# First step of both MLPs' down product by seven half-size products, with another rotation of the weight slots

## The chip, the core and the metric

One NeuronCore of one Trainium2 chip runs the whole program. The time is device microseconds of one execution; lower is better. The engines are TensorE (PE in the profile; its weight loads are PEld), VectorE (DVE), ScalarE (ACT), GpSimd (POOL) and SyncE (SP), whose queue issues nearly all the DMAs.

## The reference, cut to what matters

A sequence of 512 tokens with 1024 features goes through two transformer layers (attention over selected keys, then gated linear attention), each with an MLP, and through a third layer with a gated MLP. All is float32. The change touches the two MLPs:

```python
def squared_relu_mlp(x, w_up, w_down):
    return jnp.square(jax.nn.relu(x @ w_up)) @ w_down      # w_up 1024 x 4096, w_down 4096 x 1024
...
        h = layer_norm(DN_ALPHA * h + squared_relu_mlp(h, mlp_w_up[i], mlp_w_down[i]), ln_mlp_g[i], ln_mlp_b[i])
```

A condition vector of the third layer, `silu(c) @ w_ada + b_ada` (1024 x 6144), doesn't depend on x. The kernel works it off piece by piece between other things.

## The kernel before, in words

**Precision.** Each float32 operand is split into a high part (a rounded copy, type float32r) and a low part (the rest). A product is three matmuls: high x high, low x high, high x low. ACT makes the high part, DVE the low part by a subtraction (`raw - high`). This holds for weights (`wh`, `wl`, 128x2048) and for the hidden activations (`uh`, `ul`).

**Weights.** All weights come in chunks of 1 MB, in the order of a list (`weight_plan`, L205). A chunk is fetched into one of three `raw` buffers in turn, and split into one of the weight slots 0 to 3 (`wh`/`wl` twice, `wh2`/`wl2`, `wh3`/`wl3`). Which slot is the plan's to say, by `slots(...)`. A condition chunk ("ada" in the code, `w_ada`) takes no slot: DVE multiplies it and adds it up into `acc` (L2235, L2238), and the table `ADA` says where in the list such chunks stand. Each engine walks the same list with a cursor. DVE's handles a pair (condition chunk, weight chunk) with the weights first.

**An MLP** has 8 steps n of 512 hidden columns. The up product of a step is two chunks (q = 0, 1) of 48 matmuls each, 128x512 (`gemm_T`, L765 to L767). ACT then applies relu and square to four tiles `rb` (128x512 f32, inside `A`). The down product of hidden step d runs on PE one step later, behind the up product of step d+1.

**The down product in seven products.** Steps d = 1 to 6 see their operands as 2 x 2 blocks and use seven products of half size, P1 to P7, instead of eight (`fold`, L935). PE takes them in the order P1, P2, P6, P5, P7, P4, P3, each with 12 matmuls (L960 to L962), so 84 in a step. The extra work is sums:
- of the hidden blocks, four in a row on POOL (`hidden_sums`, L3404; L3407, L3409, L3413, L3415), released by the low part of P1's operand. They overwrite `rb`, and ACT and DVE split their results for P6, P7, P5 and P3 (`high_of` L1619, `low_half_of` L2437);
- of the weight blocks, on DVE (`weight_sums`, `last_weight_sum`, L2451 to L2464). A step has four weight parts: X and Z are fetched, Y and W are the sums. P1 and P2 use X, P6 and P4 use Y, P5 uses W, P7 and P3 use Z;
- of the results: P1, P6 and P7 go into one chain of banks, and P6 may begin when DVE has added P1 to `h` (L2477), P7 when it has added P6. P4 and P5 keep their four banks from the first such step to the last.

**Step d = 0** was a plain product: `down_first` (L974 on PE, L2507 on DVE), 8 bank tiles of 12 matmuls, 96 in all (L986 to L988). DVE adds each tile to `ALPHA * h` (L2513) and prepares two rows of `h` for the steps to come (`corner`, L2504).

Before an MLP stands `cross`, which ends the product before and makes step n = 0 of the up product on the way. DVE also finishes the layer norm there: `affine` (L2353), eight operations on `h` and `gb`, 128x1024 f32, which the order written by hand spreads over DVE's work of the first two steps. POOL loads the next norm's gain and bias into `gb` once they are through (`load_two`, L3394).

The engines meet by semaphores only. Each engine's instructions run in the order in which its own program writes them.

Of the kernel before, what the change touches and what calls it, by code (L numbers as in the profile page):

```python
# [14 lines left out]
P = 128  # L15
T = 4
# [10 lines left out]
ADA = {0: [(0, 0, 0), (1, 0, 1), (1, 0, 1), (1, 0, 1), (1, 0, 1), (1, 0, 1), (1, 1, 1), (1, 1, 1)],  # L27
       1: [(0, 0, 0), (1, 1, 1), (0, 0, 1), (0, 0, 1), (0, 0, 1), (0, 0, 1), (0, 0, 1), (0, 0, 0)]}
# [176 lines left out]
def weight_plan(a_w_in, a_w_o, b_w_in, b_w_o, mlp_w_up, mlp_w_down, w_ada_2, w_in_2, w_out_2, w_gate_2, w_up_2, w_down_2):  # L205
# [5 lines left out]
    def slots(*numbers):  # L211
        turn[:] = numbers
# [58 lines left out]
    def plan_mlp(i):  # L271
        plan_up(i, 0)
        slots(2, 3, 0, 1)
        plan_up(i, 1)
        for c in range(2):
            plan(mlp_w_down[i], 0, 4, c * 512, 512)
            plan_adas((ADA[i][1][2] + 1 - c) // 2)
        for n in range(2, 8):
            own = 0 if n % 2 else 2
            slots(own, 3)  # L280
            plan_up(i, n)
            plan_fold("m%d" % (i + 1), n - 1, mlp_w_down[i], (n - 1) * 512, (2 - own, 1, own, 3), ADA[i][n][2])
        slots(2, 3)
        plan_down(i, 7)
# [58 lines left out]
def program(nc, x, positions, a_w_in, a_w_o, b_w_in, b_w_a2, b_b_a, b_g_norm, b_w_o, ln_mix_g, ln_mix_b,  # L343
# [4 lines left out]
    with ctx:  # L348
# [223 lines left out]
        STEPS = {"m1": (1, 6), "m2": (1, 6), "m3": (0, 3)}  # L572
# [16 lines left out]
        def freed(key, d, s):  # L589
# [3 lines left out]
            if key != "m3" and d == 1:  # L593
                return s_gemm.at((key, "u read", 0)) if s in FIRST else s_gemm.at(None)
# [98 lines left out]
        def tensor_program(pe):  # L693
# [280 lines left out]
            def down_first(key):  # L974
                for c in range(2):
                    i = cur.take(skip)
                    H, L, nk, ncol = parts(i)
                    w.wait_ge(*low_of(i))
                    w.wait_ge(*s_xlow.at((key, "u", 0)))
                    for t in range(T):  # L980
                        name = ((key, "down", 0), t, c)
                        o = bank[banks.take(name)][:, :]
                        w.wait_ge(*banks.free(name, s_act.sem))
                        for f in range(4):
                            X, Y = (v[:, FIRST[f], t * P:(t + 1) * P] for v in (UH4, UL4))
                            pe.matmul(o, X, H[:, f, :], start=f == 0, stop=False)  # L986
                            pe.matmul(o, X, L[:, f, :], start=False, stop=False)
                            step = pe.matmul(o, Y, H[:, f, :], start=False, stop=f == 3)  # L988
# [2664 lines left out]
```

## Time and profile before

| | |
|---|---|
| Median of 3 runs | 1813.71 us (1813.1 to 1814.01) |
| The profiled execution | 1814.24 us, span from first to last instruction 1812.4 us |
| Mean granted TensorE clock | 0.998 |
| PE, DVE, ACT, POOL busy | 98%, 71%, 47%, 14% of the span |
| Matmuls | 8948 |
| HBM read | 185.72 MB, 104 GB/s |
| First MLP: second up chunk, old step d = 0, next up chunk begin on PE | 276.98, 287.86, 309.62 us |

Times in a timeline count from the span's start. A line has its start, its duration, the engine, the line of the kernel, the operation, output and inputs, and in brackets the idle time before it with what ended it. Printed durations of neighbours overlap a little, since an instruction's end is seen after its successor has begun.

### The profile page before, as it was taken

Reading aid. Unit: us, or ns where it says so; the run is one execution under the profiler, and the core shown is the slowest. Engines: PE = TensorE matmul, PEld = TensorE weight load, DVE = VectorE, ACT = ScalarE, POOL = GpSimd, SP = SyncE. Lnnn points to the kernel's source line nnn. Section 1 sums busy time; section 2 is a strip of 40 time slices with the busy share of each in tenths; the row PEclk is TensorE's granted clock in tenths of the full one; section 3 lists DMA queues with packets and bytes.
Section 4 is the critical chain, followed back from the end, with each engine's and each line's share of the span. In section 5 each row is a group of like instructions: output and inputs, shape, how many; then the busy total and the mean of one; then the engine's idle time right before and its main releaser. Section 6 shows DMA issues by size and latency. Waiting matters only on the chain.

```text
span 1812.4 us, 22763 instructions
## 1 busy us (share of the span) xinstructions
PE 1780.1 (98%) x8948; PEld 1452.2 (80%) x8948; DVE 1279.4 (71%) x2069; ACT 860.4 (47%) x1340; POOL 251.6 (14%) x188
## 2 busy tenths in 40 slices
PE   9999999999999999999999999999999999999998
PEld 7775788888888888878888888778756898888886
DVE  4997566987788578476777776987667645564774
ACT  4548453454444543555444544465466453332333
POOL 0241101111210054000111111000012001110101
PEclk9999999999999999999999999999999999999999
DMA  6220404544444122141543334232201422421331
GB/s 218 70 70 31 157 24 163 185 140 139 163 167 160 47 70 70 47 144 42 186 139 116 117 120 136 71 95 93 70 25 60 139 70 70 139 73 67 116 117 47
DMA packets 120059, 189.35 MB, mean 104 GB/s; under 512 B 7800, under 2 KB 72536, under 8 KB 116880
## 3 DMA queue, kind: packets, MB, share of 16 engines
q1 hardware_dynamic: 118416, 182.81, 30.6%
q0 software_dynamic: 1392, 4.82, 0.8%
q8 instruction: 71, 1.16, 0.3%
q14 instruction: 36, 0.29, 0.0%
q10 hardware_dynamic: 144, 0.26, 0.0%
HBM read 185.72 MB, written 2.16 MB: 104 GB/s over the span
## 4 chain that ended last, share of the span: by engine, by line
PE 84%; DVE 10%; ACT 4%; issue 2%; DMA 0%; DVEq 0%; ACTq 0%
PE bank L767 11%; PE bank L765 11%; PE bank L766 11%; PE bank L960 6%; PE bank L962 6%; PE bank L961 6%; PE bank L739 3%; PE bank L741 3%; PE bank L740 3%; PE bank L1049 2%; PE bank L1033 2%; PE bank L1024 2%; DVE gb L2735 2%; PE bank L862 2%; PE bank L863 2%
## 5 line engine op out<-in xcount | busy, mean ns | idle before, releaser
L2252 DVE TENSOR_TENSOR wl<-raw,wh 128x2048 fp32r<-128x2048 f32 (+2 forms) x164 | 362.5, 2213 | 115.9 <-ACT wh L1487 115.7
L1487 ACT ACTIVATE wh<-raw 128x2048 fp32r<-128x2048 f32 x169 | 308.9, 1837 | 254.3 <-PE bank L962 62.3
L765 PE MATMUL bank<-xh,wh 128*128 128x512 f32 (+1 forms) x872 | 340.4, 390 | 0.0
L767 PE MATMUL bank<-xl,wh 128*128 128x512 f32 (+1 forms) x872 | 340.0, 390 | 0.0
L766 PE MATMUL bank<-xh,wl 128*128 128x512 f32 (+1 forms) x872 | 340.0, 390 | 0.0
L765 PEld LDWEIGHTS bank<-xh,wh 128*128 128x128 f32 (+1 forms) x872 | 163.7, 188 | 34.9 <-issue 0.8
L767 PEld LDWEIGHTS bank<-xl,wh 128*128 128x128 f32 (+1 forms) x872 | 163.7, 188 | 34.6
L766 PEld LDWEIGHTS bank<-xh,wl 128*128 128x128 f32 (+1 forms) x872 | 163.7, 188 | 34.4
L960 PE MATMUL bank<-wh,uh 128*128 128x512 f32 x432 | 168.4, 390 | 0.0
L962 PE MATMUL bank<-wh,ul 128*128 128x512 f32 x432 | 168.1, 389 | 0.0
L961 PE MATMUL bank<-wl,uh 128*128 128x512 f32 x432 | 168.1, 389 | 0.0
L2477 DVE TENSOR_TENSOR h<-h,bank 128x512 f32<-128x512 f32 x132 | 86.7, 682 | 80.9 <-PE bank L962 80.9
L739 PE MATMUL bank<-wh,xh 128*128 128x512 f32 (+1 forms) x352 | 138.0, 392 | 0.5 <-DVE wl L2252 0.5
L741 PE MATMUL bank<-wh,xl 128*128 128x512 f32 (+1 forms) x352 | 134.0, 381 | 0.0
L740 PE MATMUL bank<-wl,xh 128*128 128x512 f32 (+1 forms) x352 | 133.9, 380 | 0.0
L1629 ACT ACTIVATE A<-bank 128x512 f32<-128x512 f32 x64 | 38.1, 596 | 158.8 <-PE bank L767 142.6
L3407 POOL TENSOR_TENSOR A<-A 128x512 f32<-128x512 f32 x16 | 22.7, 1417 | 590.7 <-DVE ul L2437 590.7
L960 PEld LDWEIGHTS bank<-wh,uh 128*128 128x128 f32 x432 | 81.1, 188 | 19.2 <-issue 2.5
L962 PEld LDWEIGHTS bank<-wh,ul 128*128 128x128 f32 x432 | 81.1, 188 | 16.8
L961 PEld LDWEIGHTS bank<-wl,uh 128*128 128x128 f32 x432 | 81.1, 188 | 16.9
L1619 ACT ACTIVATE uh<-A 128x512 fp32r<-128x512 f32 x112 | 64.3, 620 | 49.7 <-PE bank L962 23.0
L1581 ACT ACTIVATE A<-bank 128x512 f32<-128x512 f32 (+4 forms) x106 | 51.4, 489 | 71.4 <-PE bank L741 31.9
(413 smaller groups left out, 3431.6 us busy)
## 6 DMA issues: line engine op xcount, KB each, us to landing
raw<-in_mlp_w_up SPq DMA_DIRECT2D x32, 1024.0 KB, 6.0
raw<-in_mlp_w_down SPq DMA_DIRECT2D x32, 1024.0 KB, 5.0
raw<-in_w_ada SPq DMA_DIRECT2D x24, 1024.0 KB, 5.0
raw<-in_b_w_in SPq DMA_DIRECT2D x12, 1024.0 KB, 5.2
raw<-in_w_gate SPq DMA_DIRECT2D x11, 1024.0 KB, 5.4
raw<-in_w_up SPq DMA_DIRECT2D x11, 1024.0 KB, 5.4
raw<-in_w_down SPq DMA_DIRECT2D x11, 1024.0 KB, 5.1
raw<-in_w_in SPq DMA_DIRECT2D x10, 1024.0 KB, 5.1
```

Of the source, the lines that this page charges most:

```text
L739: pe.matmul(o, X, H[:, k, :], start=kk == 0, stop=False)
L740: pe.matmul(o, X, L[:, k, :], start=False, stop=False)
L741: step = pe.matmul(o, Y, H[:, k, :], start=False, stop=kk == 7)
L765: pe.matmul(o, H[:, k, c], xh[:, k, :], start=k == 0, stop=False)
L766: pe.matmul(o, L[:, k, c], xh[:, k, :], start=False, stop=False)
L767: step = pe.matmul(o, H[:, k, c], xl[:, k, :], start=False, stop=k == 7)
L960: pe.matmul(o, X, H[:, k0 + k, :], start=not begun and k == 0, stop=False, skip_group_check=on)
L961: pe.matmul(o, X, L[:, k0 + k, :], start=False, stop=False, skip_group_check=on)
L962: step = pe.matmul(o, Y, H[:, k0 + k, :], start=False, stop=ends and k == 1, skip_group_check=on)
L1487: act.activation(slots[slot_of[i]][0][:, 0:n], raw_of(i)[:, 0:n], ACT.Copy).then_inc(*s_high.up(i))
L2252: dve.tensor_tensor(L[:, 0:n], raw_of(i)[:, 0:n], H[:, 0:n].bitcast(F), ALU.subtract).then_inc(*s_low.up(i))
L2477: dve.tensor_tensor(hv, hv, ps, ALU.add).then_inc(*s_row.up(name, ((key, "down", 6), t, c)))
```

## The change

Step d = 0 of both MLPs goes by the seven products too. `down_first` is gone on PE and DVE. The plan calls `plan_fold` for it, ACT, DVE and POOL get their parts of a seven-product step with d = 0, and the four held banks are held from d = 0 on. The slots rotate by a table, `HOMES`. The first step's condition chunks are fewer, later steps have one more, with the same number in all. The rows of `h` are multiplied by ALPHA where the first addition to each comes, and the corners are arranged for that. At the end of an MLP the last two weight chunks lie in slots 3 and 2 instead of 2 and 3.

```diff
-ADA = {0: [(0, 0, 0), (1, 0, 1), (1, 0, 1), (1, 0, 1), (1, 0, 1), (1, 0, 1), (1, 1, 1), (1, 1, 1)],
-       1: [(0, 0, 0), (1, 1, 1), (0, 0, 1), (0, 0, 1), (0, 0, 1), (0, 0, 1), (0, 0, 1), (0, 0, 0)]}
+ADA = {0: [(0, 0, 0), (1, 0, 0), (1, 0, 1), (1, 0, 1), (1, 1, 1), (1, 0, 1), (1, 1, 1), (1, 1, 1)],
+       1: [(0, 0, 0), (1, 0, 0), (0, 0, 1), (1, 0, 1), (0, 0, 1), (1, 0, 1), (0, 0, 1), (0, 0, 0)]}
+HOMES = [(2, 3, 0, 2, 3), (3, 0, 2, 3, 0), (2, 0, 3, 2, 0), (3, 0, 2, 3, 0), (2, 0, 3, 2, 0), (3, 0, 2, 3, 0), (2, 0, 3, 2, 0)]
...
     def plan_mlp(i):
         plan_up(i, 0)
-        slots(2, 3, 0, 1)
-        plan_up(i, 1)
-        for c in range(2):
-            plan(mlp_w_down[i], 0, 4, c * 512, 512)
-            plan_adas((ADA[i][1][2] + 1 - c) // 2)
-        for n in range(2, 8):
-            own = 0 if n % 2 else 2
-            slots(own, 3)
+        for n in range(1, 8):
+            u0, u1, X, Y, W = HOMES[n - 1]
+            slots(u0, u1)
             plan_up(i, n)
-            plan_fold("m%d" % (i + 1), n - 1, mlp_w_down[i], (n - 1) * 512, (2 - own, 1, own, 3), ADA[i][n][2])
-        slots(2, 3)
+            plan_fold("m%d" % (i + 1), n - 1, mlp_w_down[i], (n - 1) * 512, (X, 1, Y, W), ADA[i][n][2])
+        slots(3, 2)
         plan_down(i, 7)
...
-        STEPS = {"m1": (1, 6), "m2": (1, 6), "m3": (0, 3)}
+        STEPS = {"m1": (0, 6), "m2": (0, 6), "m3": (0, 3)}
...
                 for n in range(1, 8):
                     for q in range(2):
                         gemm_T((key, "up", n, q), x_key)
-                    if n == 1:
-                        down_first(key)
-                    else:
-                        fold(key, n - 1)
+                    fold(key, n - 1)
...
                 for i in range(4):
                     relu(0, i // 2, i % 2)
-                    w.wait_ge(*s_act.at((key, "square", 0, i)))
-                    act.activation(UH4[:, FIRST[i], :], rb[:, i, :], ACT.Copy).then_inc(*s_xhigh.up((key, "u", 0, i)))
...
+                high_of(key, 0, P4)
+                high_of(key, 0, P1)
+                high_of(key, 0, P2)
+                for n in range(1, 8):
...
-                for i in range(4):
-                    w.wait_ge(*s_xhigh.at((key, "u", 0, i)))
-                    dve.tensor_tensor(UL4[:, FIRST[i], :], rb[:, i, :], UH4[:, FIRST[i], :].bitcast(F), ALU.subtract).then_inc(
-                        *s_xlow.up((key, "u4", 0, i), (key, "u", 0)))
+                for i, s in enumerate((P4, P1, P2)):
+                    low_half_of(key, 0, s)
                     affine(x_key, i, n_gb)
-                for q in range(2):
-                    cur.take(low)
-                    affine(x_key, 4 + 2 * q, n_gb)
-                    affine(x_key, 5 + 2 * q, n_gb)
...
+                affine(x_key, 3, n_gb)
+                for n in range(1, 8):
...
                     ada_sum()
+                    if n == 1:
+                        for i in range(4, 8):
+                            affine(x_key, i, n_gb)
+                        for t in (2, 3):
+                            corner_less(t)
...
             load_two(ln_mix_g[0], ln_mix_b[0])
+            hidden_sums("m1", 0)
             w.wait_ge(*s_row.at(("x1", "h", T - 1)))
             load_two(ln_mlp_g[0], ln_mlp_b[0])
```

In the last step ACT also makes its last copy of hidden values ahead of the last weights, and DVE takes the last weights behind the corners and P4's additions, ahead of P3's.

**DVE, first MLP, behind the third subtraction of the first hidden values.** `ul` is a low part of hidden values, `wl` of weights (with `wh3` those of the second up chunk), `h<-h,gb` an affine operation, L2235 (after: L2201) the condition chunk. Before:

```order
L2353 TENSOR_TENSOR h<-h,gb 128x1024
L2522 TENSOR_TENSOR ul<-A,uh 128x512 [waits s_xhigh]
L2353 TENSOR_TENSOR h<-h,gb 128x1024 [waits s_row]
L2252 TENSOR_TENSOR wl3<-raw,wh3 128x2048 [waits s_high,s_raw2]
L2235 TENSOR_SCALAR A<-raw,small 128x2048 [waits s_mm,s_raw1]
L2353 TENSOR_TENSOR h<-h,gb 128x1024 [waits s_turn]
L2353 TENSOR_TENSOR h<-h,gb 128x1024 [waits s_row]
L2252 TENSOR_TENSOR wl<-raw,wh 128x2048 [waits s_high,s_raw0]
```

The change, with line numbers lower by 34 on DVE from here on:

```order
L2319 TENSOR_TENSOR h<-h,gb 128x1024
L2319 TENSOR_TENSOR h<-h,gb 128x1024 [waits s_row]
L2218 TENSOR_TENSOR wl3<-raw,wh3 128x2048 [waits s_high,s_raw2]
L2201 TENSOR_SCALAR A<-raw,small 128x2048 [waits s_mm,s_raw1]
L2319 TENSOR_TENSOR h<-h,gb 128x1024 [waits s_turn]
L2319 TENSOR_TENSOR h<-h,gb 128x1024 [waits s_row]
L2319 TENSOR_TENSOR h<-h,gb 128x1024
L2319 TENSOR_TENSOR h<-h,gb 128x1024 [waits s_row]
L2474 TENSOR_TENSOR h<-h 128x512
L2474 TENSOR_TENSOR h<-h 128x512 [waits s_row]
L2403 TENSOR_TENSOR ul<-A,uh 128x512 [waits s_xhigh] x4
L2218 TENSOR_TENSOR wl<-raw,wh 128x2048 [waits s_high,s_raw0]
```

The weights of the second up chunk now stand behind three subtractions and four affine operations in place of four pairs, and before X's weights (the last row) stand four affine operations, the corners (L2474) and the four subtractions of the hidden sums.

**DVE, first MLP, behind the first down weights.** Before, with L2513 the additions of the plain product:

```order
L2437 TENSOR_TENSOR ul<-A,uh 128x512 [waits s_xhigh]
L2513 SCALAR_TENSOR_TENSOR h<-h,bank7 128x512 [waits s_gemm]
L2513 SCALAR_TENSOR_TENSOR h<-h,bank2 128x512 [waits s_gemm]
L2513 SCALAR_TENSOR_TENSOR h<-h,bank0 128x512 [waits s_gemm]
L2513 SCALAR_TENSOR_TENSOR h<-h,bank4 128x512 [waits s_row,s_gemm]
L2437 TENSOR_TENSOR ul<-A,uh 128x512 [waits s_xhigh] x2
```

The change: the sums of weights (`raw<-raw`), then the parts Z and Y, and the additions of P1 (L2447):

```order
L2417 TENSOR_TENSOR raw<-raw 128x1024 [waits s_raw1]
L2420 TENSOR_TENSOR raw<-raw 128x1024 [waits s_step,s_low]
L2422 TENSOR_TENSOR raw<-raw 128x1024 [waits s_step]
L2218 TENSOR_TENSOR wl<-raw,wh 128x2048 [waits s_high]
L2430 TENSOR_TENSOR raw<-raw 128x1024 [waits s_low]
L2218 TENSOR_TENSOR wl2<-raw,wh2 128x2048 [waits s_high]
L2447 SCALAR_TENSOR_TENSOR h<-h,bank7 128x512 [waits s_gemm]
L2447 SCALAR_TENSOR_TENSOR h<-h,bank2 128x512 [waits s_gemm]
L2403 TENSOR_TENSOR ul<-A,uh 128x512 [waits s_xhigh]
L2218 TENSOR_TENSOR wl3<-raw,wh3 128x1024 [waits s_high]
```

Two subtractions of full weight parts, one of a half part (`wl3`, W) and four sums of weights are added, and they stand ahead of or between the additions.

**POOL, first MLP, behind the loads of the first norm's gain and bias.** Before, with L3407 to L3415 the sums of d = 1:

```order
L3394 DMA gb<-in_ln_mix_g 128x1024 [waits s_mm]
L3395 DMA gb<-in_ln_mix_b 128x1024
L3394 DMA gb<-in_ln_mlp_g 128x1024 [waits s_row]
L3395 DMA gb<-in_ln_mlp_b 128x1024
L3407 TENSOR_TENSOR A<-A 128x2x256 [waits s_xlow]
```

The change, with the sums of d = 0 (L3368 to L3376) ahead of the second pair of loads:

```order
L3355 DMA gb<-in_ln_mix_g 128x1024 [waits s_mm]
L3356 DMA gb<-in_ln_mix_b 128x1024
L3368 TENSOR_TENSOR A<-A 128x2x256 [waits s_xlow]
L3370 TENSOR_TENSOR A<-A 128x2x256 [waits s_pool]
L3374 TENSOR_TENSOR A<-A 128x2x256 [waits s_pool,s_xlow]
L3376 TENSOR_TENSOR A<-A 128x2x256 [waits s_pool]
L3355 DMA gb<-in_ln_mlp_g 128x1024 [waits s_row]
```

Four sums are added, released by DVE's subtraction (s_xlow).

## Rows read from the trace of the kernel before

**Rows 1.** The page's first part: busy time, share of the span and instructions.
```profile
PE 1780.1 (98%) x8948; PEld 1452.2 (80%) x8948; DVE 1279.4 (71%) x2069; ACT 860.4 (47%) x1340; POOL 251.6 (14%) x188
```

**Rows 2.** Waits of PE over the span: line waited for, total us, times, longest.
```profile
PE bank L1175 <- DVE A L2796: 3.6, 5, 1.1
...
PE bank L1088 <- DMA C<-in_cst: 2.6, 1, 2.6
```

**Rows 3.** Timeline of PE, first MLP: start us, us, engine, line, operation.
```profile
276.98 0.39 PE L765 MATMUL bank<-xh,wh 128*128 128x512 f32 x1
...
287.86 0.39 PE L986 MATMUL bank<-wh,uh 128*128 128x512 f32 x1
...
309.62 0.39 PE L765 MATMUL bank<-xh,wh 128*128 128x512 f32 x1
...
331.37 0.39 PE L960 MATMUL bank<-wh,uh 128*128 128x512 f32 x1
```

**Rows 4.** Timeline of PE and DVE, second MLP, the same two places.
```profile
869.51 0.39 PE L765 MATMUL bank<-xh,wh 128*128 128x512 f32 x1
...
864.09 2.29 DVE L2252 TENSOR_TENSOR wl<-raw,wh 128x2048 fp32r<-128x2048 f32 x1
```

**Rows 5.** Timeline of ACT, first MLP, the last pair of squares and copies.
```profile
266.54 0.63 ACT L1632 ACTIVATE A<-A 128x512 f32<-128x512 f32 x1
...
267.20 0.63 ACT L1645 ACTIVATE uh<-A 128x512 fp32r<-128x512 f32 x1
...
269.02 0.63 ACT L1645 ACTIVATE uh<-A 128x512 fp32r<-128x512 f32 x1
```

**Rows 6.** Timeline of DVE, first MLP, up to the second weight chunk.
```profile
267.86 0.69 DVE L2522 TENSOR_TENSOR ul<-A,uh 128x512 fp32r<-128x512 f32 x1 [2.12 <-ACT uh L1645]
...
268.47 1.22 DVE L2353 TENSOR_TENSOR h<-h,gb 128x1024 f32<-128x1024 f32 x1
...
271.56 2.29 DVE L2252 TENSOR_TENSOR wl<-raw,wh 128x2048 fp32r<-128x2048 f32 x1
...
273.77 1.28 DVE L2235 TENSOR_SCALAR A<-raw,small 128x2048 f32<-128x2048 f32 x1
```

**Rows 7.** Timeline of POOL and DVE together, first MLP, at 300 to 308 us.
```profile
300.31 1.67 POOL L3407 TENSOR_TENSOR A<-A 128x512 f32<-128x512 f32 x1 [13.94 <-DVE ul L2437]
...
300.75 3.38 DVE L2252 TENSOR_TENSOR wl<-raw,wh 128x2048 fp32r<-128x2048 f32 x1
...
302.06 3.23 POOL L3409 TENSOR_TENSOR A<-A 128x512 f32<-128x512 f32 x1
...
306.80 1.29 POOL L3415 TENSOR_TENSOR A<-A 128x512 f32<-128x512 f32 x1
```

**Rows 8.** Timeline of POOL and DVE, first MLP, at 381 to 387 us.
```profile
381.69 2.91 POOL L3413 TENSOR_TENSOR A<-A 128x512 f32<-128x512 f32 x1 [0.49 <-POOL A L3409]
...
383.37 3.38 DVE L2238 SCALAR_TENSOR_TENSOR A<-raw,small,A 128x2048 f32<-128x2048 f32 x1
```

**Rows 9.** Timeline of DVE, weight sums of a seven-product step, to its first addition.
```profile
323.88 1.22 DVE L2451 TENSOR_TENSOR raw<-raw 128x1024 f32<-128x1024 f32 x1 [0.28 <-DMA raw<-in_mlp_w_down]
...
331.08 2.28 DVE L2252 TENSOR_TENSOR wl<-raw,wh 128x2048 fp32r<-128x2048 f32 x1
...
333.28 0.68 DVE L2477 TENSOR_TENSOR h<-h,bank 128x512 f32<-128x512 f32 x1
```

**Rows 10.** The page's DMA issues: out<-in, queue, count, KB, us to landing.
```profile
raw<-in_mlp_w_down SPq DMA_DIRECT2D x32, 1024.0 KB, 5.0
```

**Rows 11.** The page's costliest groups: busy us, mean ns; idle before, releaser.
```profile
L1487 ACT ACTIVATE wh<-raw 128x2048 fp32r<-128x2048 f32 x169 | 308.9, 1837 | 254.3 <-PE bank L962 62.3
```

**Rows 12.** Timeline of DVE, end of the second MLP.
```profile
1150.95 2.29 DVE L2252 TENSOR_TENSOR wl<-raw,wh 128x2048 fp32r<-128x2048 f32 x1 [0.43 <-ACT wh L1487]
...
1153.44 0.68 DVE L2425 TENSOR_TENSOR h<-h,bank 128x512 f32<-128x512 f32 x1
```

**Rows 13.** A stretch by PE, PEld, DVE, ACT, POOL busy, PEclk, DMA share, GB/s.
```profile
617.00:620.40 3.40, 3.40 (x10) 2.63 (x9) 3.40 (x3) 2.87 (x2) 0.00 (x0) 0.50 0.00 0
```

More of the change, by code:

```diff
@@ L592, in freed @@
                 return s_gemm.at(("o3", T - 1, 1))
-            if key != "m3" and d == 1:
-                return s_gemm.at((key, "u read", 0)) if s in FIRST else s_gemm.at(None)
+            if d == 0 or d == 1 and s == P4:
+                return s_gemm.at(None)
             return s_gemm.at((key, "P", d - 2, s, 1)) if s == P4 else s_gemm.at((key, "P", d - 1, s, 1))
@@ L972, in fold @@
                 ada_turn()
[L974 to L988, printed above, removed]
-                        step.then_inc(*s_gemm.up(name, *([("chunk", i)] if t == T - 1 else [])))
-                s_gemm.mark((key, "u read", 0))
             def mlp(key, x_key):
@@ L2466, in mlp @@
             def mlp(key, x_key, n_gb):
-                last = {(t, c): ((key, "down", 0), t, c) for t in range(T) for c in range(2)}
+                last = {(t, c): (x_key, "h", t) for t in range(T) for c in range(2)}
+                scaled = set()
                 def last_low(i):
@@ L2497, in lasting, with corner_less, corner_more @@
                             banks.read[where] = s_row.at(name)
-                def corner(t, op, name):
-                    hv = h[:, t, 512:1024]
+                def corner_less(t):
+                    hv, name = h[:, t, 512:1024], (key, "less", t)
+                    w.wait_ge(*s_row.at(last[t, 0]))
+                    dve.tensor_tensor(hv, hv, h[:, t, 0:512], ALU.subtract).then_inc(*s_row.up(name))
+                    last[t, 1] = name
+                def corner_more(t):
+                    hv, name = h[:, t, 512:1024], (key, "more", t)
                     w.wait_ge(*s_row.at(last[t, 0]))
                     w.wait_ge(*s_row.at(last[t, 1]))
-                    dve.tensor_tensor(hv, hv, h[:, t, 0:512], op).then_inc(*s_row.up(name, ((key, "down", 6), t, 1)))
+                    dve.scalar_tensor_tensor(hv, hv, ALPHA, h[:, t, 0:512], ALU.mult, ALU.add).then_inc(
+                        *s_row.up(name, ((key, "down", 6), t, 1)))
+                    scaled.add((t, 1))
                     last[t, 1] = name
-                def down_first(c):
-                    for t in range(T):
-                        name = ((key, "down", 0), t, c)
-                        hv = h[:, t, c * 512:(c + 1) * 512]
-                        w.wait_ge(*s_gemm.at(name))
-                        w.wait_ge(*s_row.at((x_key, "h", t)))
-                        dve.scalar_tensor_tensor(hv, hv, ALPHA, bank[banks.of[name]][:, :], ALU.mult, ALU.add).then_inc(*s_row.up(name))
-                        banks.read[name] = s_row.at(name)
                 def owed():
```

38 lines of the change are left out of this document (10 added, 28 removed).

## Prediction

> **What bounds the kernel now.** I read the busy shares first: TensorE (PE) is busy for 98% of the span, VectorE (DVE) for 71%, GpSimd (POOL) for 14% [rows 1]. Then the waits of PE: the largest sum is 3.6 us, the longest single wait 2.6 us, at the very start, and none lies in an MLP step [rows 2]. So the span is PE work, and a matmul left out saves its pitch as long as nobody comes late with its operands. The pitch is in the PE timeline: from the first matmul of the old down step at 287.86 to the first behind it at 309.62 are 96 matmuls, 21.76 us, so 0.2267 us each; a chunk of the up product (48) takes 10.88 us, from 276.98 to 287.86 [rows 3]. The same two places of the second MLP lie 592.53 us later, on PE and on DVE [rows 4]. So one MLP is worked out and doubled.
>
> **What is removed.** Per MLP 96 matmuls become 7 products of 12, so 84: 12 x 0.2267 = 2.72 us less on PE, 5.4 in all. This is the whole gain, and it is PE time, so it counts in full if PE never waits.
>
> **What is added and moved, on DVE.** The list that DVE must finish before the third product (P6) can begin becomes longer, and it begins later. All durations are start to start, which is 0.08 below the printed ones (an ul subtraction printed 0.69 has its successor after 0.61 [rows 6]).
>
> - *Start.* The copies now stand behind all four squares. In the old order the copy of the third quarter stands between its square and the next relu [rows 5]: 0.66 us from square to copy. Without it the last square's copy begins at 269.02 - 0.66 = 268.36, and DVE's subtraction 0.66 behind it (267.20 to 267.86 [rows 5, 6]): 269.01. DVE has nothing to do before, though its old queue had begun its four pairs seven us earlier.
> - *Up to the weights of the second up chunk.* Three subtractions (0.61 each) and four affine operations (1.21 each) are 6.67 us, then the weight subtraction, printed 2.29 [rows 6]: 275.68 to 277.97. It stood at 271.56 [rows 6]. PE wants these weights at 276.98 [rows 3]: a wait of 1.0 us.
> - *GpSimd's four sums now fall into this list.* They are released by the subtraction of P1, and take 1.29 us each when alone [rows 7]. Beside DVE they don't share, they alternate: POOL began at 300.31, DVE's weight subtraction took 3.38 instead of 2.29, and the next POOL sum stretched to 3.23, which ends 1.2 us after DVE's [rows 7]. Again at 381.69: the POOL sum ran 2.91, and the DVE operation behind it 3.38 [rows 8]. So a sum put between two DVE operations with two SBUF sources delays the second by 3.38 - 2.29 = 1.09 us. Here behind P1's subtraction come only such operations (affine, subtraction, affine, affine, weights), one sum gets between each two: 4 x 1.09 = 4.4 us. The wait at the second up chunk becomes 5.35 us; it ends at 282.33.
> - *From there to the first product.* The condition chunk 1.20, four affine operations 4.84, two corners and four ul subtractions 6 x 0.61 = 3.66 (the corners have the ul's shape), the weights of X 2.21: 11.9 us. They end at 294.24; PE is through the up chunk at 282.33 + 10.88 = 293.2: a wait of 1.0 us.
> - *From there to the third product.* The sums and weights of an existing step take 323.88 to 331.08, 7.20 us, and 2.20 more for Y, then the first addition 0.68 [rows 9]. So P6 may begin at 294.16 + 7.20 + 2.20 + 0.68 = 304.24. PE has done P1 and P2 (5.44 us) at 299.7: a wait of 4.55 us.
>
> Together 5.35 + 1.0 + 4.55 = 10.9 us of waits per MLP, less 2.72: **8.2 us lost per MLP**, 16.4 in all. Checked from the other end: DVE's list from 269.01 is 30.9 us, with GpSimd 35.2, and PE would want P6 at 287.86 + 5.44 = 293.3, after 24.3.
>
> **The port rule against the row.** The rows show the alternation for weight subtractions and for the accumulation of a condition chunk [rows 7, 8]; no row has a GpSimd sum beside an affine operation, which also reads two SBUF tensors. That it is held too is my choice, since its kind of operands is the same; if only the weights' subtraction were held, 3.3 of the 4.4 us would go, and if nothing were, all of them. The Trainium skill, "SBUF — State Buffer", section "Who interferes with whom", says that a DVE instruction with two SBUF inputs contends with a GpSimd instruction that reads SBUF, and that the loser blocks until the other is done. By that rule the sum is the one above, without it 8.7 us less for both MLPs; the trace agrees where it has rows (3.38 against 2.29).
>
> **Behind P6.** W's subtraction comes 2.4 us behind the first addition, at 306.5, and P5 wants it at 307.0; P7 wants P6's addition at 309.7, about when it comes. Both cost nothing, and there is half a microsecond of cover. After the step DVE is some 2 us behind PE; an existing step has Y's weights at 333.3, 3.5 us before P6 wants them (331.37 + 5.44) [rows 3, 9], so the next one takes that up: nothing.
>
> **DMA and queues.** SP asks for Z once the condition chunk in its buffer is used, at 283.5, and it lands 5.0 us later [rows 10], before 294: nothing. The LN loads on POOL now stand behind its sums, done by 281, before the last affine operation releases them: nothing. The other slot rotation: the last weights of each MLP go where Y was, so their copy waits for the sixth product instead of the fourth. That is 2.72 us before the step's end, and PE wants them 2.72 us behind it: 5.44 us for a copy of 1.84 [rows 11] and a subtraction of 2.29. PE doesn't wait, but DVE's next work is pushed. At the end of the second MLP DVE had only 0.43 us of idleness before the next weights [rows 12]. Bounds 0 and 2.2 us (one weight subtraction); I take 0.7, because most of it falls into idle time of the same queue.
>
> **TensorE's clock.** Waits of 5.35 and 4.55 us are longer than any here (2.6, [rows 2]). It did fall once: from 617.0 to 620.4 us it stands at 0.50, 1.2 instead of 2.4 GHz, where PE had a few slow matmuls and little weight loading [rows 13]. So I estimate a fall at 3.4 us of half speed, at most 1.7 us. Four long waits (two per MLP) bound this at 0 and 6.8. I take one fall, 1.7: the nearest row, the wait of 2.6 us, brought none, but these are twice as long.
>
> **Sum.** 1814.24 (the profiled execution) + 16.4 + 0.7 + 1.7 = 1833.0. That execution is 0.5 above the median of the three runs, so **1832.5 us**.
>
> **The rivals.**
>
> - *A, the affine operations aren't held by GpSimd* (nothing is). For it: no row of them beside a sum. Against: they have the operands of those that were. The waits are 1.0 + 1.0 + 4.55 = 6.5 us per MLP, less 2.72: 3.8, twice 7.7, with 0.7 at the end and no fall: 1822.1 us.
> - *B, the gain survives.* The place is DVE's list before P6. If PE finds its operands in time, 1813.7 - 5.4 = 1808.3 us. It decides where the list of 30.9 us fits into the 24.3 us that PE gives it, by work done in the idle time before 269.0; for it speaks DVE's 71% [rows 1], against it that the queue is in order and its first entry waits for the last square.
> - *C, the clock falls in each long wait*: 1831.3 + 6.8 - 0.5 = 1837.6 us.
> - *D, waits and saving cancel*, about 2.7 us of waits per MLP, between A and B: 1813.7 us.
>
> **How the numbers follow.** The forecast gets 0.76, A 0.12, B 0.05, C 0.05, D 0.02. What a measurement of this kernel can tell from no change is 0.2%, 3.6 us. Faster by more is B, 0.05; within it is D, 0.02; slower are the forecast, A and C, 0.93. The range takes in A below and C above: 1820.5 to 1839.
>
> **What would show it.** In the profile of the changed kernel: PE waits on the weights of the second up chunk in each MLP, near 5 us (1 in case A); on Y's weights or the first addition, near 4.5 us; about 1 us at X's weights. GpSimd's first four sums of each MLP stretch to 2 us and more, and affine operations print 2.3 instead of 1.22. PE's count is 24 lower. The forecast is wrong if PE has no wait over 2 us in the MLPs, or if later steps wait too.

## The result, and the profile after

| | before | changed |
|---|---|---|
| Median | 1813.86 us (1813.1 to 1816.81, 4 runs) | 1835.38 us (1833.5 to 1837.03, 4 runs) |
| Profiled execution, span | 1814.24, 1812.4 us | 1833.50, 1831.7 us |
| Granted clock | 0.998 | 0.994 |

The ratio is 1.0116, 95% interval 1.0103 to 1.0128: slower, by 21.5 us. The profiled execution was forecast at 1833.0 and took 1833.5. Two of the four runs took 1837.0, at a granted clock of 0.993 and 0.991, so the median lies 2.9 us above the forecast one.

PE's waits come first again: over the whole span, line waited for, total, times, longest. Before, no MLP step had one of over 2 us [rows 2].

```profile
PE bank L762 <- DVE wl L2218: 9.8, 2, 4.9
PE bank L957 <- DVE h L2447: 6.1, 2, 3.1
PE bank L1256 <- DVE xl L2254: 3.1, 4, 1.2
```

Two new lines, two waits each, one in each MLP. In the timeline of PE, first MLP, they stand at the weights of the second up chunk and at the first addition, as forecast. The rows are: the last matmul ahead of the first wait, the one behind it, the begin of the first product, the last of the second, P6's first behind its wait, and the first of the next step's up product.

```profile
277.13 0.39 PE L764 MATMUL bank<-xl,wh 128*128 128x512 f32 x1
282.44 0.80 PE L762 MATMUL bank<-xh,wh 128*128 128x512 f32 x1 [4.92 <-DVE wl L2218]
...
295.72 0.39 PE L957 MATMUL bank<-wh,uh 128*128 128x512 f32 x1
...
300.93 0.39 PE L959 MATMUL bank<-wh,ul 128*128 128x512 f32 x1
304.32 0.75 PE L957 MATMUL bank<-wh,uh 128*128 128x512 f32 x1 [3.00 <-DVE h L2447]
...
319.65 0.39 PE L762 MATMUL bank<-xh,wh 128*128 128x512 f32 x1
```

The first up chunk of n = 1 begins at 266.45 and the next step's at 319.65: 53.20 us, where it was 43.55. That is +9.65: 12 matmuls less (-2.72), the stop at the second chunk (277.33 to 282.44, +5.11), that chunk in 13.28 us in place of 10.88 (+2.40), the stop ahead of P6 (+3.16), and its last 60 matmuls in 15.33 us in place of 13.60 (+1.73). The second MLP has the same within 0.1: 867.35 to 920.49, +9.59.

The two terms with nothing but slow matmuls are the clock. Below are windows of the first MLP (columns as in [rows 13]): one behind the first stop and one behind the second stand at half the clock, the one between them at the full one. Read in finer windows, the half clock lasts from 280.45, still inside the first stop, to 287.28, and from 304.35 to 307.76.

```profile
283.00:286.40 3.40, 3.40 (x9) 2.64 (x8) 3.37 (x4) 0.00 (x0) 0.00 (x0) 0.50 0.45 118
287.50:295.00 7.50, 7.50 (x34) 6.19 (x33) 7.50 (x9) 2.35 (x4) 1.10 (x2) 1.00 0.92 307
304.40:307.40 3.00, 3.00 (x7) 2.38 (x8) 3.00 (x5) 0.27 (x1) 0.20 (x1) 0.50 0.93 298
```

DVE in the same place, from its first subtraction to the weights that PE waits for, and further on the first addition; below, POOL's four sums.

```profile
269.40 0.69 DVE L2403 TENSOR_TENSOR ul<-A,uh 128x512 fp32r<-128x512 f32 x1 [8.00 <-ACT uh L1595]
270.01 1.22 DVE L2319 TENSOR_TENSOR h<-h,gb 128x1024 f32<-128x1024 f32 x1
...
272.88 1.79 DVE L2403 TENSOR_TENSOR ul<-A,uh 128x512 fp32r<-128x512 f32 x1
274.60 4.52 DVE L2319 TENSOR_TENSOR h<-h,gb 128x1024 f32<-128x1024 f32 x2
279.04 3.35 DVE L2218 TENSOR_TENSOR wl<-raw,wh 128x2048 fp32r<-128x2048 f32 x1
...
303.50 1.28 DVE L2447 SCALAR_TENSOR_TENSOR h<-h,bank 128x512 f32<-128x512 f32 x2
```

```profile
271.92 2.21 POOL L3368 TENSOR_TENSOR A<-A 128x512 f32<-128x512 f32 x1 [71.38 <-DVE ul L2403]
274.21 1.61 POOL L3370 TENSOR_TENSOR A<-A 128x512 f32<-128x512 f32 x1
275.96 2.08 POOL L3374 TENSOR_TENSOR A<-A 128x512 f32<-128x512 f32 x1
278.12 2.13 POOL L3376 TENSOR_TENSOR A<-A 128x512 f32<-128x512 f32 x1
```

DVE stands idle for 8.00 us, then its list runs to P6 with no gap over 0.15 us. Three of its rows are stretched: the subtraction of P2 by 1.10 over 0.69, two affine operations (4.52) by 2.05 over 2.47, the weights by 1.06 over 2.29. 4.2 us in all, and POOL's sums fill just these places.

At the end of the second MLP the wait on ACT's tile was 0.66 us before. In the changed kernel it is 1.35:

```profile
1188.92 2.13 PE L804 MATMUL bank<-C,A 128*128 128x128 f32 x16 [1.35 <-ACT A L1583]
```

The spans differ by 19.3 us: 9.65 and 9.59 in the MLPs, 0.69 here, 0.38 ahead of the first MLP, -1.28 between the two, and 0.27 behind. The -1.28 isn't in the forecast: the clock fall of [rows 13], 1.7 us, is missing from this profiled execution; behind that place PE waits 1.0 us at L736, where it didn't, and 0.8 us less at the line that heads [rows 2]. The last section shows that this fall is there in some variants of the changed kernel and not in others.

### The profile page after: what moved, and what is told of

Read it like the earlier page. It is cut to its first block, busy times and chain, and to the rows that moved or that the text cites. A ratio compares the mean times of both kernels' runs of the same rounds, so it can differ in the third digit from the quotient of the medians.

```text
span 1831.7 us, 22763 instructions
## 1 busy us (share of the span) xinstructions
PE 1782.5 (97%) x8924; PEld 1452.7 (79%) x8924; DVE 1311.7 (72%) x2091; ACT 869.0 (47%) x1350; POOL 268.8 (15%) x196
## 4 chain that ended last, share of the span: by engine, by line
PE 80%; DVE 14%; ACT 4%; issue 2%; DMA 0%; DVEq 0%; ACTq 0%
PE bank L764 10%; PE bank L762 10%; PE bank L763 10%; PE bank L957 6%; PE bank L958 6%; PE bank L959 6%; PE bank L736 3%; PE bank L738 3%; PE bank L737 3%; DVE wl L2218 2%; PE bank L1025 2%; PE bank L1009 2%; PE bank L1000 2%; DVE gb L2696 2%; PE bank L859 2%
## 5 line engine op out<-in xcount | busy, mean ns | idle before, releaser
L2218 DVE TENSOR_TENSOR wl<-raw,wh 128x2048 fp32r<-128x2048 f32 (+1 forms) x168 | 370.2, 2206 | 103.6 <-ACT wh L1463 103.6
L1463 ACT ACTIVATE wh<-raw 128x2048 fp32r<-128x2048 f32 (+2 forms) x173 | 314.5, 1828 | 254.9 <-PE bank L959 68.8
L957 PE MATMUL bank<-wh,uh 128*128 128x512 f32 x488 | 191.9, 393 | 6.1 <-DVE h L2447 6.1
L958 PE MATMUL bank<-wl,uh 128*128 128x512 f32 x488 | 191.1, 392 | 0.0
L959 PE MATMUL bank<-wh,ul 128*128 128x512 f32 x488 | 190.8, 391 | 0.0
L736 PE MATMUL bank<-wh,xh 128*128 128x512 f32 (+1 forms) x352 | 138.1, 392 | 1.5 <-DVE wl L2218 1.5
L3368 POOL TENSOR_TENSOR A<-A 128x512 f32<-128x512 f32 x18 | 26.4, 1464 | 751.8 <-DVE ul L2403 751.8
L957 PEld LDWEIGHTS bank<-wh,uh 128*128 128x128 f32 x488 | 92.4, 189 | 28.5 <-DVE wl L2218 6.9
L959 PEld LDWEIGHTS bank<-wh,ul 128*128 128x128 f32 x488 | 92.4, 189 | 19.4
L958 PEld LDWEIGHTS bank<-wl,uh 128*128 128x128 f32 x488 | 92.5, 190 | 19.1
L2403 DVE TENSOR_TENSOR ul<-A,uh 128x512 fp32r<-128x512 f32 x126 | 87.8, 737 | 20.6 <-ACT uh L1595 20.5
L1595 ACT ACTIVATE uh<-A 128x512 fp32r<-128x512 f32 x126 | 72.2, 620 | 58.7 <-POOL A L3374 24.1
```

Of the source, the lines that this page charges most:

```text
L736: pe.matmul(o, X, H[:, k, :], start=kk == 0, stop=False)
L957: pe.matmul(o, X, H[:, k0 + k, :], start=not begun and k == 0, stop=False, skip_group_check=on)
L958: pe.matmul(o, X, L[:, k0 + k, :], start=False, stop=False, skip_group_check=on)
L959: step = pe.matmul(o, Y, H[:, k0 + k, :], start=False, stop=ends and k == 1, skip_group_check=on)
L1463: act.activation(slots[slot_of[i]][0][:, 0:n], raw_of(i)[:, 0:n], ACT.Copy).then_inc(*s_high.up(i))
L2218: dve.tensor_tensor(L[:, 0:n], raw_of(i)[:, 0:n], H[:, 0:n].bitcast(F), ALU.subtract).then_inc(*s_low.up(i))
```

## Experiments

Eleven kernels, numbered as they were planned. Theory L says that the changed kernel is bound by DVE's list from the last square to the first addition: whatever stands in it counts, GpSimd's sums too.

**Affine operations first (e1).**

```diff
-                for i, s in enumerate((P4, P1, P2)):
-                    low_half_of(key, 0, s)
-                    affine(x_key, i, n_gb)
-                affine(x_key, 3, n_gb)
+                for i in range(8):
+                    affine(x_key, i, n_gb)
+                for s in (P4, P1, P2):
+                    low_half_of(key, 0, s)
...
                     if n == 1:
-                        for i in range(4, 8):
-                            affine(x_key, i, n_gb)
                         for t in (2, 3):
                             corner_less(t)
```

> The changed kernel with all eight affine operations of the layer norm ahead of the first three subtractions of hidden values, nothing else. In the changed kernel VectorE is idle for 8.0 us before the first of these subtractions (269.40), and the affine operations' inputs are there. Theory L (VectorE's list sets the begin of the third product; everything that stands in it costs, GpSimd's sums included, and PE's stops ahead of it are only its shadow): 9.7 us leave the list, 1.6 of them come back since they don't all fit into the 8.0. The wait at the second up chunk goes from 4.92 to under 0.5 us, the one before the third product becomes 2.5 to 3.2 us, with perhaps one clock fall (1.7) behind it. Per MLP -2.7 + 2.9 + 0 to 1.7, so 0 to 2 us; the kernel takes 1815 to 1819 us. Rival P (the seven products at d = 0 cost by themselves, whatever the order): stays at 1833 to 1837 us.

Measured: 1818.59 us (7 runs), ratio 1.0027 (1.0015 to 1.0039). The stop at the second up chunk is gone, the one at P6 is 2.61 us in both MLPs.

```profile
261.88 9.66 DVE L2319 TENSOR_TENSOR h<-h,gb 128x1024 f32<-128x1024 f32 x8
271.46 1.89 DVE L2403 TENSOR_TENSOR ul<-A,uh 128x512 fp32r<-128x512 f32 x3
273.27 3.39 DVE L2218 TENSOR_TENSOR wl<-raw,wh 128x2048 fp32r<-128x2048 f32 x1
276.58 2.31 DVE L2201 TENSOR_SCALAR A<-raw,small 128x2048 f32<-128x2048 f32 x1
278.81 3.48 DVE L2474 TENSOR_TENSOR h<-h 128x512 f32<-128x512 f32 x2
```

The eight affine operations, 1.20 each, nearly fit into the old gap: the subtractions begin 4.4 us behind the first up chunk's begin (267.04 to 271.46) in place of 2.95. 17 of the 21.5 us are gone by the operations' place alone: rival P is out. The sums now stretch the weights, the condition chunk (TENSOR_SCALAR with one SBUF tensor as source, 2.31 in place of 1.28) and the two corners (3.48 in place of 1.29).

**GpSimd's sums later (e2).**

```diff
             def hidden_sums(key, d):
+                if d == 0 and key != "m3":
+                    w.wait_ge(*low_of(folds[key, 0][0] - 1))
```

> The changed kernel, with GpSimd's first sum of each MLP waiting for VectorE's subtraction of the second up chunk's weights, so that the four sums stand beside later operations. Theory L: the wait at the second up chunk shrinks from 4.92 to 0.6 to 1.2 us and no clock fall follows it, but the list is as long as before (the sums alternate with the affine operations behind it), so PE only stops later: a new wait of 3 to 5 us in front of the first down product, the third product begins at the same place within 1 us (37.9 us behind the first up chunk), and the total stays at 1831 to 1836 us. Rival W (each wait and each clock fall counts for itself): 4.3 us of wait and 2.4 us of half clock less per MLP, 1820 us. Rival N (GpSimd and VectorE don't exclude each other; the 4.52 us for two affine operations have another cause): the wait at the second up chunk doesn't shrink.

Measured: 1834.17 us, ratio 1.0109 (1.0093 to 1.0125).

```profile
274.96 2.28 DVE L2218 TENSOR_TENSOR wl<-raw,wh 128x2048 fp32r<-128x2048 f32 x1
277.16 1.28 DVE L2201 TENSOR_SCALAR A<-raw,small 128x2048 f32<-128x2048 f32 x1
278.35 9.01 DVE L2319 TENSOR_TENSOR h<-h,gb 128x1024 f32<-128x1024 f32 x4
```

```profile
PE bank L957 <- DVE wl L2218: 9.5, 2, 4.8
PE bank L957 <- DVE h L2447: 3.9, 2, 2.2
...
PE bank L762 <- DVE wl L2218: 1.4, 2, 0.7
```

The early stop shrinks from 4.92 to 0.70, and PE stops for 4.75 us at X's weights instead. Four affine operations take 9.01 us where they took 4.87 in the changed kernel (4.1 more, about what the stretched rows there made). From DVE's first subtraction to the first addition are 34.0 us (268.48 to 302.48), in the changed kernel 34.1. Theory L to the point; W is out, since 4.2 us less of a wait gave nothing. Where PE stops isn't what costs.

**The sums shortened (e11).** They cover 32 of the 256 columns of each block in d = 0; the rest of the hidden sums is left out.

```diff
+                cut = 32 if d == 0 and key != "m3" else 256
...
-                pool.tensor_tensor(quad(0, 0), quad(0, 0), quad(0, 1), ALU.subtract).then_inc(*s_pool.up((key, "S", d, P7)))
+                pool.tensor_tensor(quad(0, 0)[:, :, 0:cut], quad(0, 0)[:, :, 0:cut], quad(0, 1)[:, :, 0:cut], ALU.subtract).then_inc(*s_pool.up((key, "S", d, P7)))
...
```

> The changed kernel, with GpSimd's four sums of d = 0 in both MLPs over 32 of the 256 columns of each block alone (the rest of the hidden sums is left out), and everything else as it was: VectorE's list has the same instructions, only GpSimd holds it for less. Theory L with exclusion (a sum between two operations delays the second by about what it has left to do): nearly all of the 4.4 us of stretching goes. The two affine operations print 2.4 together instead of 4.52, the weights' subtraction 2.3 instead of 3.35; the wait at the second up chunk falls from 4.92 to 1.0 to 1.6 us, the third product begins 3.4 to 4.2 us earlier behind the first up chunk than in the changed kernel (37.9 there). The sum of waits and clock falls per MLP goes from 12.4 to 7 to 9: 1822 to 1828 us. Rival N (the stretching is no exclusion but a fixed cost of each instruction of GpSimd, or has another cause): it stays, and so do 1833 us.

Measured: 1828.44 us, ratio 1.0074 (1.0059 to 1.0090), 0.4 us above the range that L gave.

```profile
273.44 2.61 DVE L2319 TENSOR_TENSOR h<-h,gb 128x1024 f32<-128x1024 f32 x2
275.98 2.41 DVE L2218 TENSOR_TENSOR wl<-raw,wh 128x2048 fp32r<-128x2048 f32 x1
```

```profile
PE bank L957 <- DVE h L2447: 8.7, 2, 4.3
PE bank L762 <- DVE wl L2218: 2.2, 2, 1.1
PE bank L957 <- DVE wl L2218: 1.2, 2, 0.6
```

Same instructions, same places, only the sums' length differs, and the stretching goes. P6 begins 34.04 us behind the first up chunk (266.28 to 300.32) in place of 37.87: 3.83 us of the 4.2. So it was the sums that held the affine operations (rival A is out), and by their length, not by a fixed cost of each (rival N is out). The three waits, 1.1, 0.6 and 4.3, are those of the forecast without its 4.4 (1.0, 1.0, 4.55).

**Corners and half of the affine operations behind P6 (e3).**

```diff
-                    if n == 1:
-                        for i in range(4, 8):
-                            affine(x_key, i, n_gb)
-                        for t in (2, 3):
-                            corner_less(t)
...
                         added(d, P6)
+                        if n == 1:
+                            for i in range(4, 8):
+                                affine(x_key, i, n_gb)
+                            for t in (2, 3):
+                                corner_less(t)
```

> The changed kernel with the last four affine operations and the two corners behind the addition of the sixth hidden sum's product (P6) in place of before the hidden sums' subtractions: 4 x 1.21 + 2 x 0.61 = 6.06 us leave the list before the third product. Theory L: the wait at the second up chunk stays (4.9 us, and the 2.4 us of half clock behind it, which now nothing covers any more), those before the first and the third product are gone. Per MLP 5.1 + 2.4 - 2.7 = +4.8 us, the kernel takes 1823 to 1826 us. Rival Q (behind P6 is no room: the operations push the next step's weights): a new wait of 1 to 4 us at the second step's up chunks, 1826 to 1832 us.

Measured: 1832.85 us, ratio 1.0101 (1.0085 to 1.0117), 7 us above my theory's range and 0.9 above rival Q's. Q's mechanism holds and my theory's number falls: the stop at P6 is gone, but in the first MLP PE stops for 3.83 us at the next step's up chunk, for a bank that P7's addition leaves late, and behind it the clock falls again (60 matmuls in 16.44 us in place of 13.6).

```profile
304.39 4.87 DVE L2319 TENSOR_TENSOR h<-h,gb 128x1024 f32<-128x1024 f32 x4
309.17 1.29 DVE L2474 TENSOR_TENSOR h<-h 128x512 f32<-128x512 f32 x2
310.38 3.74 DVE L2218 TENSOR_TENSOR wl<-raw,wh 128x2048 fp32r<-128x2048 f32 x1
314.04 3.35 DVE L2204 SCALAR_TENSOR_TENSOR A<-raw,small,A 128x2048 f32<-128x2048 f32 x1
317.31 1.27 DVE L2447 SCALAR_TENSOR_TENSOR h<-h,bank 128x512 f32<-128x512 f32 x2
```

The list has a second deadline behind P6: P7's addition (317.31) frees a bank that PE wants at 314.14. And DVE's delay brings its weights and the condition chunk beside the next step's sums (3.74, 3.35). In the changed kernel two of these sums ran while DVE stood idle for 3.54 us, and the same two operations took 2.29 and 2.35:

```profile
313.77 2.29 DVE L2218 TENSOR_TENSOR wl<-raw,wh 128x2048 fp32r<-128x2048 f32 x1 [3.54 <-ACT wh L1463]
```

In the second MLP, whose step has no condition chunk there, the stop is 0.76.

**Into the gap (e4).** On POOL the second sum also waits for the last square, since the first now runs ahead of it.

```diff
                 for i in range(4):
                     relu(0, i // 2, i % 2)
-                high_of(key, 0, P4)
-                high_of(key, 0, P1)
+                    if i == 1:
+                        high_of(key, 0, P1)
+                high_of(key, 0, P4)
                 high_of(key, 0, P2)
...
-                for i, s in enumerate((P4, P1, P2)):
-                    low_half_of(key, 0, s)
-                    affine(x_key, i, n_gb)
-                affine(x_key, 3, n_gb)
+                affine(x_key, 0, n_gb)
+                affine(x_key, 1, n_gb)
+                low_half_of(key, 0, P1)
+                for i in range(2, 5):
+                    affine(x_key, i, n_gb)
+                low_half_of(key, 0, P4)
+                low_half_of(key, 0, P2)
...
```

The last three affine operations and the corners stand behind P6's addition, as in e3.

> Both ideas and one more: ScalarE copies P1's hidden values right behind the second square, VectorE does two affine operations, P1's subtraction and three more affine operations in the 8.0 us in which it stood idle, GpSimd's first sum falls into the same gap (its second waits for the last square), and the last three affine operations and the corners stand behind P6's addition. Theory L: first addition ready at about 292 where PE wants the third product at 293.6; no wait over 0.5 us and no clock fall in d = 0 of either MLP. The saving of 12 matmuls per MLP remains in full: 1814.2 - 5.4 + 0.7 (end of the second MLP) = 1809.5 us, 1807.5 to 1811. Rival Q (the work moved behind P6 shows in the second step): 1811 to 1818 us. Rival P (the seven products at d = 0 cost by themselves): 1830 us or more.

Measured: 1817.02 us (10 runs), ratio 1.0013 (1.0003 to 1.0022), outside my theory's range and inside rival Q's. The second MLP has no wait in d = 0. The first has none ahead of P6, but e3's at the next step:

```profile
306.94 0.39 PE L959 MATMUL bank<-wh,ul 128*128 128x512 f32 x1
310.56 0.47 PE L762 MATMUL bank<-xh,wh 128*128 128x512 f32 x1 [3.23 <-DVE h L2448]
```

Behind it the clock falls once more (the next chunk pair takes 23.47 us in place of 21.76). So rival Q again, in one MLP.

**All eight in the gap (e5), P7's addition first (e6), both (e7).** e5 moves the last three affine operations of e4 into the gap too. e6 changes in e4:

```diff
                         added(d, P6)
...
-                        weights(q1 - 1)
-                        added(d, P7)
+                        if n == 1:
+                            added(d, P7)
+                            weights(q1 - 1)
...
```

> The kernel e4_into_the_gap with the last three affine operations in the gap as well (ahead of the subtractions for P4 and P2); only the two corners are left behind P6's addition. Theory L: in e4 the stop of 3.23 us at the second step's first up chunk came from P7's additions, which stood behind three affine operations, two corners, a stretched weight subtraction and a condition chunk; with 3.6 us less ahead of them it is gone. In exchange the list ahead of the third product begins 3.1 us later than in e4 and loses 1.5 us of idle time: first addition at about 294, PE wants P6 at 293.6, so waits of 0.3 to 1.5 us per MLP in all, perhaps at the second up chunk (weights at 277 to 278, wanted at 277.2). 1810 to 1813 us. Rival R (the stop in e4 comes from the GpSimd sums of step 1, not from what was moved): the wait at the second step's up chunk stays over 2 us, 1814 us or more.

> The kernel e4_into_the_gap, where in the first step P7's additions stand ahead of the next up chunk's weights and the condition chunk instead of behind both. Theory L: the additions end at 304.1 instead of 310.6, so the banks are free in time; the weights of the second step's first up chunk then end at 307.7 where PE wants them at 307.1: a wait of 0.3 to 1 us in the first MLP, no clock fall. 1815.0 - 2.6 - 1.7, so e4 less 4 to 5 us: 1809.5 to 1812 us. Rival R (as above: the time is lost to GpSimd's sums of step 1, whatever the order): a wait of 2 to 4 us on the weights or the additions remains, 1814 us or more.

> e5 and e6 together: eight affine operations in the gap, corners behind P6's addition, P7's additions ahead of the next weights. Theory L: as e5, 0.3 to 1.5 us of waits per MLP ahead of the third product and none at the second step; 1810 to 1813 us. It beats e6 only if the second step is what costs, and loses to it if the list ahead of P6 is.

Measured (10 runs each): e5 1813.15 us, ratio 0.9998 (0.9988 to 1.0007); e6 1810.41 us, 0.9978 (0.9969 to 0.9988); e7 1813.95 us, 0.9996 (0.9987 to 1.0005). e5's profile shows P6 waiting 1.26 us in both MLPs and 0.67 at the next step in the first, e7's the two of 1.26 alone. e5 and e7 lie 0.15 and 0.95 us above their ranges, and which of the two is better can't be told from the medians: e7's profile has a clock fall between the MLPs (see the last section) that e5's doesn't have. The part from the first MLP's next step to the second MLP's n = 1 takes 550.1 us in e7 and 547.9 in e5, while d = 0 of the first MLP is 0.8 us shorter in e7. **e6 is faster than the kernel before.** Its DVE where P7's addition was moved:

```profile
297.79 3.61 DVE L2320 TENSOR_TENSOR h<-h,gb 128x1024 f32<-128x1024 f32 x3
301.32 1.29 DVE L2475 TENSOR_TENSOR h<-h 128x512 f32<-128x512 f32 x2
302.52 1.28 DVE L2448 SCALAR_TENSOR_TENSOR h<-h,bank 128x512 f32<-128x512 f32 x2
303.72 2.56 DVE L2219 TENSOR_TENSOR wl<-raw,wh 128x2048 fp32r<-128x2048 f32 x1
```

And PE from the first up chunk of n = 1 to the next step's, without a wait:

```profile
266.19 0.40 PE L762 MATMUL bank<-xh,wh 128*128 128x512 f32 x1
...
307.01 0.39 PE L762 MATMUL bank<-xh,wh 128*128 128x512 f32 x1
```

40.82 us, which is 180 matmuls at 0.2267. The saving of 2.72 us per MLP is real and whole, once DVE comes in time.

**The end of an MLP (e8, and e9 with e6).** Y and W of the last seven-product step change slots, and the last weights get their old place in the orders.

```diff
-HOMES = [(2, 3, 0, 2, 3), (3, 0, 2, 3, 0), (2, 0, 3, 2, 0), (3, 0, 2, 3, 0), (2, 0, 3, 2, 0), (3, 0, 2, 3, 0), (2, 0, 3, 2, 0)]
+HOMES = [(2, 3, 0, 2, 3), (3, 0, 2, 3, 0), (2, 0, 3, 2, 0), (3, 0, 2, 3, 0), (2, 0, 3, 2, 0), (3, 0, 2, 3, 0), (2, 0, 3, 0, 2)]
...
                         lasting(P5, 0, 1, False)
                         last_low(2)
                         added(d, P7)
+                        weights(q1)
                         last_low(3)
...
                         lasting(P4, 2, 0, True)
-                        weights(q1)
                         added(d, P3)
```

> e7, and at the end of each MLP the parts Y and W of the last seven-product step change slots (Y into the slot that the second last up chunk's weights leave, W into the first's), so that the last weight chunk waits for the fourth product instead of the sixth, with the old order of ScalarE and VectorE there. Theory L: the wait on ScalarE's tile behind the second MLP, 1.35 us with the new rotation and 0.66 with the old one, goes back to 0.7, so 0.7 us less than e7 in the profile, under what the medians can tell. Rival S (that wait has nothing to do with the slots): it stays at 1.35.

> The kernel e6_p7_added_first with the slots and the order at the end of each MLP as in e8_end_rotation. Both MLPs run without a wait in d = 0, as in e6: per MLP 40.8 us from the first up chunk of n = 1 to that of n = 2, 2.72 less than before. The wait behind the second MLP goes from 1.35 to 1.1 us, as from e7 to e8. So within 0.5 us of e6: 1809.5 to 1811.5 us, and faster than the kernel before by 0.15 to 0.25%. If the end's order pushes other work of VectorE (the rival), the wait behind the second MLP is above 1.35 us or a new one stands before it: 1812 us or more.

Measured: e8 (e7 with it) 1814.57 us, 0.9998 (0.9989 to 1.0007); e9 1810.81 us (11 runs), 0.9981 (0.9972 to 0.9989). The wait behind the second MLP is 1.08 us in e8 and 1.09 in e9, after 1.34 in e7 and 1.35 in e6. So a quarter of a microsecond of the 0.7 belongs to the slots and the order together (e8 changes both), and neither L's 0.7 nor S's 1.35 came out; where the other 0.4 comes from stays open. e9 can't be told from e6.

**The other half of the change alone (e10).** The kernel before with the new rotation from n = 2 on, the new condition chunks and the new end; step d = 0 stays plain.

```diff
-            own = 0 if n % 2 else 2
-            slots(own, 3)
+            u0, u1, X, Y, W = HOMES[n - 1]
+            slots(u0, u1)
...
-        slots(2, 3)
+        slots(3, 2)
         plan_down(i, 7)
```

> The kernel before with only the other half of the change: the new rotation of the slots from n = 2 on, the new table of condition chunks, the last weights in slots 3 and 2 with their later place in ScalarE's and VectorE's orders; step d = 0 stays a plain product of 96 matmuls. Theory L: nothing of this stands ahead of a waiting PE but at the end of the second MLP: 0.7 us there, 1814 to 1816 us. Rival V (the rotation itself makes later weights wait, and part of the 19 us is its): 1817 us or more, with waits on weights in the steps n = 2 to 7.

Measured: 1815.19 us (10 runs), ratio 1.0005 (0.9996 to 1.0014). In the profile PE waits 1.34 us behind the second MLP, as in the changed kernel, and nowhere anew, so rival V (later weights wait, part of the 19 us is the rotation's) is out. The median can't tell it from no change; the profile shows 0.7 us.

## Why the prediction was right, point by point

- *The saving.* 12 matmuls per MLP, 2.72 us, in full: e6.
- *Start of DVE's list.* Forecast 2.94 us behind the first up chunk's begin, measured 2.95 (266.45 to 269.40).
- *GpSimd's four sums.* Forecast 4.4 us, 4.2 in the profile, 3.83 gained by e11. That the affine operations are held as the weights' subtractions were [rows 7] was my choice by operand kind, and right. The Trainium skill, "SBUF — State Buffer", section "Who interferes with whom", says that a DVE instruction with two SBUF inputs contends with a GpSimd instruction that reads SBUF. The rows here agree (4.52 against 2.47 for two affine operations). The condition chunk in e1, with one SBUF tensor as source and another small one for the factor, is stretched as well (2.31 against 1.28). Alone it takes little more than half the time of a two-source subtraction of its size (1.28 against 2.29); whether that has to do with it, no run here shows.
- *The stop at the second up chunk.* Forecast 5.35, measured 5.11 with the gap of one matmul in it (4.92 printed).
- *X's weights and P6.* Forecast 1.0 and 4.55, measured 0 and 3.16. DVE's times came as forecast (P6 begins 37.87 us behind the first up chunk, forecast 38.17). PE came later, 2.4 us for the slow chunk, so it waited less. In e11, where no slow chunk lies between the stops, the two are 0.6 and 4.3.
- *The clock.* Here the count was off, and it is the mis-sized term. The clock added 3.4 us to the time where I had 1.7. I took one fall of 1.7 us for both MLPs. There were four, two in each. The two behind the first stop (2.40 and 2.33 us) cost nothing, since PE would have waited for DVE anyway; the two behind P6 cost 1.73 and 1.67. Rival C had the falls right and their price wrong: it added all four. DVE's list, which runs on through the first fall, shows that the price is hidden there.
- *The row that I took for no fall.* I called the wait of 2.6 us one that brought none. It can't stand for that. It lies at the very start of the execution, and the 14 matmuls behind it took 3.25 us, where 26 of the same line took 3.00 a little later: twice as long each, although the printed granted clock is 1.00 in both places. Half speed is what these rows look like, so the count of one fall rested on a misread row.

```profile
2.64 3.25 PE L1088 MATMUL bank<-C 128*128 128x128 f32 x14 [2.64 <-DMA C<-in_cst]
...
6.71 3.00 PE L1088 MATMUL bank<-C 128*128 128x128 f32 x26
```

- *Behind P6.* Forecast nothing, and nothing came in the changed kernel. The half microsecond of cover that I named is that of P5 and P7. Ahead of the next step's weights DVE has 3.54 us of idle time in the changed kernel. e3 and e4 put 6.1 and 4.8 us of work there, the sums stretched what came behind it, and 3.83 and 3.23 us of wait came.
- *The end of the second MLP.* Forecast 0.7, measured 0.69, and e10 shows that it belongs to the rotation's half. The size is luck: 0.7 was picked between 0 and 2.2. That slots and order make up all of it isn't borne out (e8).
- *Rivals.* A is out by e11; B isn't what the changed kernel does, but e6 comes near it (1810.4, where B gave 1808.3): its condition, work done in the idle time ahead of the list, is met there, and part of the list stands behind P6 besides. D didn't occur.

Sum by these terms: 2 x (5.11 + 2.40 + 3.16 + 1.73 - 2.72) = 19.4, and 0.7: 20.1 us against 18.8 forecast. That the profiled execution came within 0.5 us of its forecast is partly luck: these terms are 1.3 us too low in the forecast, and the rest of the span, the missing clock fall above all, made up for 0.6 of it.

## What to carry to other kernels

A saving on the bounding engine is worth what the helper engine's list leaves of it: add up that list from its release to its deadline, with every instruction that stands in its order, and look for idle time ahead of the release in which some of it could be done. Two waits of the bounding engine that hang on one list aren't priced one by one: together they come to what the last deadline is missed by. What is taken from the earlier one comes back at the later (e2), and a clock fall behind the earlier one is covered by the later wait. Work moved behind a deadline needs the next deadline looked up first.

## What was not expected

- In these kernels each of the stops of PE from 3.0 to 4.9 us in d = 0 and at the step behind it was followed by a stretch at half the granted clock. The shorter ones went either way, read from the 60 matmuls behind the stop (13.6 us at the full clock): none behind 1.26 us (e5, e7, e8); none behind 1.64 us (e2, first MLP), with 13.84; a fall behind 2.23 us (e2, second), with 15.33; behind 2.61 us (e1) none in the first MLP, with 13.84, and a fall in the second, with 15.33.
- The fall of [rows 13], in a place without a stop, comes and goes. In the profiled executions it lasts 3.4 us before and in e2, e3 and e10, 6.8 us in e4, e6, e7, e8 and e11, and is absent in the changed kernel, e1, e5 and e9. What PE did before it fell is the first row below, from the kernel before: eight matmuls of 16 rows in 3.69 us, with the weight loads busy for 1.22 of 3 us (614 to 617). The changed kernel has the same stretch, 1.22 of 3 us (624 to 627), without a fall. So why it falls in one execution and not in another stays open. It is about the size of what an experiment of this kind wants to tell apart, so a comparison of two profiles has to look for it.

```profile
612.98 3.69 PE L1158 MATMUL bank<-A 16*128 16x512 f32 x8
```

```profile
612.00:615.00 3.00, 3.00 (x6) 0.81 (x5) 1.92 (x4) 1.01 (x1) 0.00 (x0) 0.70 0.52 203
615.00:618.00 3.00, 3.00 (x8) 2.33 (x9) 3.00 (x3) 2.31 (x2) 0.00 (x0) 0.50 0.00 0
618.00:621.00 3.00, 3.00 (x11) 2.37 (x10) 2.97 (x3) 2.80 (x2) 0.00 (x0) 0.67 0.67 184
```

The second three are windows of e6. The time lost in them is 0.30, 0.50 and 0.33 of 3 us each, 3.4 us in all, where the 3.4 us at half the clock in [rows 13] lost 1.7. That is the clock alone. The profiles with and without it are less far apart (2.2 us from e5 to e7), since PE has a wait there without a fall (1.0 us at L736 in e5) that it hasn't with one.
